# A block of two experts moved from fourth to third place in the expert stage of a diffusion backbone

## What is computed

```python
def _swiglu(x, wg, wu, wd):
    return (jax.nn.silu(x @ wg) * (x @ wu)) @ wd
...
    routed = _grouped_experts(xt, idx, w, wg, wu, wd)
    return (routed + _swiglu(xt, sg, su, sd)).reshape(b, t, d)
```

## Time and profile before

| what | value |
|---|---|
| runs of the kernel | 2138.48, 2140.32, 2143.11 us, median 2140.32 |
| the profiled execution, its own time | 2138.53 us |
| its span from the first to the last instruction | 2136.9 us |
| mean granted TensorE clock | 0.874 |
| PE busy | 1693.5 us (79%) |
| DVE, ACT, POOL busy | 697.7, 340.2, 325.0 us |
| moved by DMA | 589.22 MB |

### The profile page before, as it was taken

One profiled execution on the slowest core, in us unless ns is written; L12 is line 12 of the kernel. 1 busy time (PEld: TensorE's weight loads), 2 busy tenths in 40 slices (PEclk: granted clock), 3 DMA queues, 4 the chain that ended last, 5 costly groups with the idle time before them and its releaser, 6 DMA issues. The chain is left out here.

```text
span 2136.9 us, 19635 instructions
## 1 busy us (share of the span) xinstructions
PE 1693.5 (79%) x7016; PEld 872.2 (41%) x7016; DVE 697.7 (33%) x1277; ACT 340.2 (16%) x767; POOL 325.0 (15%) x228
## 2 busy tenths in 40 slices
PE   3649788784999996888985478966999978898854
PEld 0117647643444442333431366634443433333321
DVE  0014245667432211111113836494322111111117
ACT  0003162000111110111111215301111111111110
POOL 0000000125111111222210300071111111111100
PEclk8779896585999998999998699976999989999987
DMA  9973001033799999999986301307899999999945
GB/s 371 428 310 124 32 11 45 0 124 150 295 369 400 413 411 399 407 401 403 400 358 252 110 11 40 116 28 293 313 402 409 398 407 414 403 384 386 381 196 234
DMA packets 108533, 589.22 MB, mean 276 GB/s; under 512 B 22577, under 2 KB 24625, under 8 KB 54801
## 3 DMA queue, kind: packets, MB, share of 16 engines
q1 hardware_dynamic: 84816, 537.55, 62.1%
q0 software_dynamic: 23616, 50.38, 6.1%
HBM read 575.09 MB, written 48.41 MB: 292 GB/s over the span
## 5 line engine op out<-in xcount | busy, mean ns | idle before, releaser
L1992 PE MATMUL bank<-weights,scratch 128*64 128x512 f32 x448 | 222.6, 655 | 83.6 <-DMA scratch<-in_moe_w_up 45.9
L2099 DVE TENSOR_TENSOR scratch<-scratch,bank 128x256 f32<-128x256 f32 x88 | 53.9, 613 | 670.7 <-ACT scratch L2067 641.9
L1993 PE MATMUL bank<-scratch 128*64 128x512 f32 x480 | 232.6, 641 | 0.0
L1992 PEld LDWEIGHTS bank<-weights,scratch 128*64 128x64 f32 x448 | 65.4, 151 | 230.3 <-issue 230.2
L1992 PE MATMUL bank<-scratch 128*64 128x512 f32 x288 | 132.2, 614 | 18.3 <-DMA scratch<-in_moe_w_up 18.3
L2067 ACT ACTIVATE scratch<-bank 128x256 f32<-128x256 f32 x88 | 33.8, 384 | 705.8 <-PE bank L1993 429.0
L1998 PE MATMUL bank<-weights,scratch 128*128 128x512 f32 x320 | 141.9, 596 | 2.5 <-ACT scratch L2062 1.7
L1993 PE MATMUL bank<-weights,scratch 128*64 128x512 f32 x256 | 122.9, 636 | 0.0
L1797 POOL DMA_INDIRECT y_rows<-hP,y_idx x42 | 43.5, 1036 | 480.9 <-DVE hP L2104 413.1
L1998 PE MATMUL bank<-scratch 128*128 128x512 f32 x256 | 112.9, 594 | 0.0
L2025 PE MATMUL bank<-scratch 128*64 128x512 f32 x240 | 109.4, 599 | 0.0
(11 more groups left out here) (318 smaller groups left out, 2807.0 us busy)
## 6 DMA issues: line engine op xcount, KB each, us to landing
weights<-in_moe_w_gate SPq DMA_DIRECT2D x64, 1024.0 KB, 14.1
weights<-in_moe_w_up SPq DMA_DIRECT2D x64, 1024.0 KB, 16.2
weights<-in_moe_w_down SPq DMA_DIRECT2D x64, 1024.0 KB, 18.5
scratch<-in_moe_w_gate SPq DMA_DIRECT2D x64, 1024.0 KB, 23.7
scratch<-in_moe_w_up SPq DMA_DIRECT2D x64, 1024.0 KB, 25.7
scratch<-in_moe_w_down SPq DMA_DIRECT2D x64, 1024.0 KB, 18.9
wmod_more<-in_w_mod SPq DMA_DIRECT2D x9, 3072.0 KB, 32.3
weights<-in_w_mod SPq DMA_DIRECT2D x7, 3072.0 KB, 32.3
```

The lines of the kernel that those rows point to most:

```text
L1992: nc.tensor.matmul(out[0:HALF, :], x[:, 0:HALF], w0[:, kk], start=(kk == 0), stop=(kk == KT - 1))
L1993: m = nc.tensor.matmul(out[HALF:P, :], x[:, HALF:P], w1[:, kk], start=(kk == 0), stop=(kk == KT - 1))
L2099: nc.vector.tensor_tensor(B.h[b % 2].rearrange("p (j q) -> p q j", j=2), B.ex[b % 2].rearrange("p (q j) -> p q j", j=2), k.ps[2 + b % 2][: ...
```

## The change

The first pair comes as third of the blocks with experts of their own, ahead of expert 2: the list now starts block 0 shared, block 1 expert 0, block 2 expert 1, block 3 the pair of positions 3 and 4, block 4 expert 2 (position 2), block 5 rank 3, and goes on as before. Positions, slots and the order of the loads stay. Since positions no longer rise along the list, `block_of` and `rank_at` become dictionaries by position, and SP takes the blocks with positions from 3 on.

```diff
@@ block_plan
     assert solo == SOLO and at == NE and len(plan) == BLOCKS
+    plan.insert(FIXED - 1, plan.pop(FIXED))
     for t, after in reversed(list(enumerate(SHARED_AFTER))):
@@ stage_experts
-    block_of = [b for b, (_, _, ranks) in enumerate(plan) for _ in ranks]
-    rank_at = [r for _, _, ranks in plan for r in ranks]
+    block_of = {at + i: b for b, (_, at, ranks) in enumerate(plan) for i in range(len(ranks))}
+    rank_at = {at + i: r for _, at, ranks in plan for i, r in enumerate(ranks)}
@@ SP's program
-            for b in routed[FIXED:]:
+            for b in [b for b in routed if plan[b][1] >= FIXED]:
```

## The result

| | median | runs, us | ratio to before, 95% interval |
|---|---|---|---|
| before, beside it | 2141.84 us | 6, from 2138.48 to 2143.11 | |
| after | 2153.61 us | 6, from 2149.83 to 2158.68 | 1.0061 [1.0045, 1.0078] |
| after, measured again | 2153.15 us, before beside it 2143.12 | 6, from 2147.33 to 2156.12 | 1.0044 [1.0031, 1.0058] |

The forecast was 2149.3 us within 2144.0 to 2153.5. The sign held, and so did the cause, SP's late issue of load 6; how much of that debt is left when PE meets it was put too low. The time lies 4.3 us above the forecast and 0.1 above the range's end. The loss is 11.8 us by the medians of the first measurement and 10.0 by those of the second, where 9.0 were forecast. The profiled execution of after took 2152.1 us, with a span of 2150.5 and a mean granted clock of 0.872.

What follows compares the result with a forecast made beforehand. The prediction took expert-weight DMA transfers as the bound, so idle engines count: load 6's late issue costs 5.0 us a layer, 4.5 after payback, 9.0 in all. 2140.3 + 9.0 = 2149.3 us, range 2144.0 to 2153.5.

Steps and rivals of the forecast that it cites:

- PE's and POOL's part: Swapped blocks: PE's order costs 0.1 us at most; POOL's third gather takes over the fourth's wait, hidden under 12 us.
- The debt is 5.0 us a layer: DMA queue: load 6's gate and up, 2.10 MB at 418 GB/s, make load 7 and all after it 5.0 us later.
- The down of load 6 costs nothing: DMA queue: this down waits until about 616.0, but queued loads keep the engines busy to 617.9, so no second hole opens.
- How much is given back: Up to block 14, idle moments repay 1.2 and 1.8 us by the mean, none by the slowest engine; 4.5 a layer left.
- Up to block 14 PE has its weights in time, so SP's issues keep their times: Both expert stages before block 14: PE has its weights in time, so SP issues its loads when it does today.
- Block 14 waits 4 to 5.4 us in both layers: Sign of being right: PE waits 4 to 5.4 us for weights at the pair of block 14 in each layer.
- The clock counts 0: Block 14's gate-up: a lower TensorE clock could add 3.4 us a layer, mostly covered by block 20's 2.94 us wait; counted 0.
- Sum 9.0: Whole kernel: 4.5 us late in each of two layers, 9.0 us in all, added to 2140.3 us.
- that the engines give back more: Rival, DMA low windows counted in bytes: 2.8 + 2.4 = 5.2 us are left, 2145.5 us; chance 0.12.
- that PE is the bound: Rival: PE has slack at block 14, later waits come from its own late releases; +0 to 1 us, about 2141; chance 0.07.
- that SP could issue load 7 at 587: Rival: the pair's early-freed slots let SP fill the hole of 594 to 600, gaining about 5 us a layer, 2130; chance 0.03.
- the clock rival: Rival: block 14's 3.4 us from a lower clock is uncovered in either layer; 9.0 + 5 to 6.8, about 2155; chance 0.08.

Runs made afterwards that it cites:

- half the debt: Kernel before with only the gate weights of load 6 asked for one block later, its up weights at the old time: 2146.66 us, ratio 1.0022.

## Why the prediction was nearly right, and where it failed

- **PE's and POOL's part costs nothing**: held to within what shows. With the slots in order of release the same swap gives 0.9994; the pair's gate-up starts at 578.93 in after, where expert 2's started at 579.72 in an execution 0.9 us later, so load 4 was there in time. The price inside PE was put at 0.1 us at most; by block 7 it is 0.35 us (626.86 - 562.28 against 627.39 - 563.16).
- **SP issues load 6 at 599**: held (598.18). The windows from 588 to 594 are empty.
- **The debt is 5.0 us a layer**: held as the cost of the late issue. The bytes that are missing behind the empty windows are about those of load 6's gate and up, and half of them cost half in layer 0 (2.4 us at block 22, against 5.0).
- **The down of load 6 costs nothing**: held in the change, where the window 612 to 616 is full; alone it costs 1.8.
- **How much is given back: the step that failed.** Between the 3.8 and 3.2 us that the mean over the engines leaves and the 5.0 of the slowest one I took 4.5 a layer, "9.0 in all", as the debt at block 14. The mean did what its sum said: 4.0 us by bytes at 680 us in layer 0. But PE doesn't see the mean. Block 14 is late, counted from load 4's issue, by 5.8 us in layer 0 and 4.8 in layer 1, in the repeat by 5.5 and 5.8, and nothing of the 5.0 is paid back at block 22 of layer 0 (5.0 and 5.2). With half the debt it is plainer still: 0.9 us by bytes, 3.2 and 2.9 at block 14. That fits the slowest engine, the upper end of the sum, 10.0: the measured 10.0 and 11.8 lie at and above it, not at the middle that I chose. The Trainium skill's page "DMA: Bandwidth & Descriptors", in the section on why a DMA increments its semaphore by 16 and not by 1, says that the engines of one DMA finish independently and that only the full count says that all data landed. By that rule the sum had been 10.0, and the starts of block 14 agree with it. No view here shows single engines, so that PE waited for the slowest one is not shown.
- **"Up to block 14 PE has its weights in time, so SP's issues keep their times"**: wrong as well. I had looked for waits and had not asked how near to one the blocks before block 14 stood. Block 8 stood within 2.7 us (5.0 - 2.31; with half the debt it doesn't wait): it now waits 2.31 us, PE and its releases are late from there, load 15 goes out at 671.27 instead of 669.27, and the low windows around 669 move on with them (668 to 670 still shows 0.89 and 670 to 672 0.87, where I had expected full ones). This isn't what undid the payback, though: with the gate alone late block 8 has no wait, load 15 keeps its time, and block 14 is late by all of the debt still.
- **Block 14 waits 4 to 5.4 us in both layers**: wrong. The waits are split between blocks 8 and 14: 2.31 and 3.09 in layer 0, 2.23 and 0.68 in layer 1, and 2.52 and 0.91, 2.05 and 3.50 in the repeat. Two of the four sums, 5.4 and 5.6, are near the forecast, and two are not, 2.9 and 3.4; in those the clock fell at block 8.
- **The clock counts 0**: held at block 22 of layer 0. In layer 1 the fall at block 14 in the repeat, 1.7 us, is still there at block 22, and 0.4 of it at the last block.
- **Sum 9.0**: 10.5 by the stages of the first profiled execution, 12.4 by the second, 10.7 and 10.8 at the last blocks, 10.0 and 11.8 by the medians. With 5.0 in place of 4.5 the sum would have been 10.0. What layer 1 loses beyond that, 6.0 to 7.0 us at its last block in four executions, the prediction had no term for, and the cause of the part that isn't the clock stays open.
- **The rivals**: that the engines give back more (5.2 left) fell with the 5.0 of layer 0; that PE is the bound fell with the waits at blocks 8 and 14; that SP could issue load 7 at 587 fell with its issue at 599.75. What is left of the clock rival is the 1.7 us at block 22 of layer 1.
- **The range**: of the 4.3 us between forecast and median, 1.5 are the base (the median of before was 2141.84 in six runs, 2140.3 in the three that I had, and 2142 to 2143 in the later measurements), and 2.8 the loss itself. On which side of the range's end the time falls is luck: the repeat's median, 2153.15, lies inside. My upper end left out half of the clock rival and had no room for the base; a median of three runs that scatter over 4.6 us deserves 1 to 2 us on either side.

## What to carry to other kernels

When blocks are reordered over a ring of buffers, ask first which issue is tied to the block that moved back: a queue that waits in order makes that one late buffer late for everything behind it, and the price here was the bytes that the idle engines would have carried, in full; the engines' later idle moments didn't pay it back for the matmuls that waited. The opposite wasn't worth the same: transfers that started sooner gained nothing while the consumer's releases set how many could follow. And before counting on slack at the first block that waits, look at each block ahead of it for how long its data had been there; block 8 had no wait and stood 2.7 us from one.

## What the runs showed of the hardware

- The fall of the clock after a wait was not all or nothing, and did not go by the length of the wait. After 3.09 and 3.50 us it came behind the first matmul and cost 1.7 us in a gate-up of 16 pairs of matmuls, where I had reckoned with 3.4; it cost about the same after 2.23 and 2.52 us, and didn't come after 2.31 and 2.94.
- The bytes moved and the start of a waiting matmul told different debts: 0.9 us by bytes and 3.2 us at block 14 for the same 1.05 MB asked for late, 117 and 149 us behind load 4's issue.
- What lies between the stages' rows differed by up to 8 us between profiled executions (from -0.7 to 7.2), and the same 433 matmuls of the attention took 78.51 to 83.10 us, at granted clocks of 0.96 and 0.89. A span difference of one execution each is no measure of a change of 0.5% here; the loss of a stage between two anchored rows agreed to 0.4 us at block 22 of layer 0 (4.8 to 5.2 in four executions), but to 1.7 at its last block (4.4 to 6.1) and to 3 in layer 1 (5.5 to 8.4).
